# Norms by halves of the tokens: the last projections of a block and the first pairs of the next run half by half, two norms in a row folded

## The reference

```
rms(x, g)  = x * rsqrt(mean(x*x) + eps) * g
x  = x + concat(spatial gating, conformer conv, gated delta rule)(rms(x, mix_g) @ w_in) @ w_out
x  = x + (silu(rms(x, ffn_g) @ w_gate) * (rms(x, ffn_g) @ w_up)) @ w_down
x  = rms(x, final_g)                                  # end of the first block
h  = concat(meta, x)
h  = h + 0.5 * swiglu(rms(h, ffn1_g))                 # d_ff 2816
h  = h + merge(window attention, state-space scan)(rms(h, mix2_g) @ w_in_2) @ w_out_2
h  = h + 0.5 * swiglu(rms(h, ffn2_g))
out = rms(h, final2_g)[:, 16:]
```

## Time and profile before

| | |
|---|---|
| median of 3 runs | 4128.43 us (4125.76 to 4130.19) |
| profiled execution, its own time | 4125.97 us |
| its span | 4124.2 us |
| TensorE busy | 3722.5 us (90%) |
| VectorE, ScalarE, GpSimd busy | 1851.9, 598.5, 1531.2 us |
| mean granted TensorE clock | 0.952 |

### The profile page before, as it was taken

The page is one execution under the profiler, slowest core; times in us unless marked ns, Lnnn a source line. Parts: engine busy times, 40 slices in busy tenths (PEclk is TensorE's granted clock), DMA queues, the critical chain, the costliest instruction groups (busy, mean ns, idle before and its releaser), DMA issues.

```text
span 4124.2 us, 52854 instructions
## 1 busy us (share of the span) xinstructions
PE 3722.5 (90%) x20662; PEld 3162.4 (77%) x20662; DVE 1851.9 (45%) x2660; ACT 598.5 (15%) x1204; POOL 1531.2 (37%) x718
## 2 busy tenths in 40 slices
PE   5977788879999998899999979998888879999997
PEld 2756578668888886899999978887666668888886
DVE  3299566452121217422222286683777762121216
ACT  3132322110000000200000012113443010000000
POOL 3333200354444443444444453322113454444443
PEclk8989899789999999999999989999999989999998
DMA  2110000111111111111111112101002311111111
GB/s 93 36 31 26 21 1 1 61 31 46 51 45 48 45 49 43 30 42 51 41 51 46 40 47 106 55 27 44 29 24 84 117 32 46 51 41 51 46 49 63
DMA packets 56807, 189.86 MB, mean 46 GB/s; under 512 B 6112, under 2 KB 6240, under 8 KB 56032
## 3 DMA queue, kind: packets, MB, share of 16 engines
q1 hardware_dynamic: 45792, 147.20, 11.8%
q10 hardware_dynamic: 10880, 40.78, 2.6%
HBM read 170.05 MB, written 16.84 MB: 45 GB/s over the span
## 4 chain that ended last, share of the span: by engine, by line
PE 73%; DVE 20%; issue 3%; ACT 2%; POOL 1%; DMA 1%; DVEq 0%; POOLq 0%; ACTq 0%
PE acc L560 21%; PE acc L561 21%; PE acc L562 21%; DVE cv_acc L1123 2%; DVE tmp L528 2%; ACT sc L1566 1%; PE acc L846 1%; DVE ssq L648 1%; PE acc L857 1%; DVE st L1790 1%; DVE cvo L1106 1%; PE acc L856 1%; DVE sq L647 1%; PE acc L497 1%; DVE rs L518 1%
## 5 line engine op out<-in xcount | busy, mean ns | idle before, releaser
L449 POOL TENSOR_TENSOR w_hi<-w_raw,consts 128x1024 fp32r<-128x1024 f32 (+3 forms) x316 | 683.8, 2164 | 2127.8 <-PE acc L562 1861.4
L560 PE MATMUL acc<-h_hi,w_hi 128*128 128x512 f32 (+2 forms) x3552 | 1321.3, 372 | 102.4 <-issue 60.0
L561 PE MATMUL acc<-h_lo,w_hi 128*128 128x512 f32 (+2 forms) x3552 | 1320.0, 372 | 0.0
L562 PE MATMUL acc<-h_hi,w_lo 128*128 128x512 f32 (+2 forms) x3552 | 1312.6, 370 | 0.0
L560 PEld LDWEIGHTS acc<-h_hi,w_hi 128*128 128x128 f32 x3552 | 674.3, 190 | 218.5 <-issue 112.5
L561 PEld LDWEIGHTS acc<-h_lo,w_hi 128*128 128x128 f32 x3552 | 672.8, 189 | 103.4 <-issue 2.7
L562 PEld LDWEIGHTS acc<-h_hi,w_lo 128*128 128x128 f32 x3552 | 673.5, 190 | 99.2
L451 POOL TENSOR_TENSOR w_lo<-w_raw,w_hi 128x1024 fp32r<-128x1024 f32 (+3 forms) x316 | 726.0, 2297 | 24.8
L614 DVE TENSOR_TENSOR ff_hi<-tmp,acc 128x512 f32 (+3 forms) x154 | 94.5, 613 | 1119.6 <-PE acc L562 1106.0
L562 PE MATMUL acc<-ff_hi,w_lo 128*128 128x512 f32 (+2 forms) x1232 | 446.8, 363 | 0.0
L560 PE MATMUL acc<-ff_hi,w_hi 128*128 128x512 f32 (+2 forms) x1232 | 446.1, 362 | 0.0
(11 more groups left out here) (301 smaller groups left out, 3647.5 us busy)
## 6 DMA issues: line engine op xcount, KB each, us to landing
w_raw<-in_ffn_w_dram SPq DMA_DIRECT2D x88, 512.0 KB, 3.5
w_raw<-in_w_in_dram SPq DMA_DIRECT2D x56, 512.0 KB, 3.6
w_raw<-in_ffn_w_dram SPq DMA_DIRECT2D x32, 384.0 KB, 3.0
w_raw<-in_w_gate_dram SPq DMA_DIRECT2D x22, 512.0 KB, 3.5
w_raw<-in_w_up_dram SPq DMA_DIRECT2D x22, 512.0 KB, 3.5
w_raw<-in_ffn_w_dram SPq DMA_DIRECT2D x32, 320.0 KB, 2.9
w_raw<-in_w_out_dram SPq DMA_DIRECT2D x16, 512.0 KB, 3.5
gates_kept<-gstage ACTq DMA_DIRECT2D x32, 256.0 KB, 2.0
```

Source lines behind the costliest of these rows:

```text
L449: own.link(pool.tensor_tensor(hi.rearrange(blocks, n=P), raw.rearrange(blocks, n=P), ones.unsqueeze(1).broadcast_to([P, seg.kt, P]), ALU.m ...
L560: pe.matmul(bank, wh, rh, start=(k == 0), stop=False)
L561: pe.matmul(bank, wh, rl, start=False, stop=False)
L562: ins = pe.matmul(bank, wl, rh, start=False, stop=(k == seg.kt - 1))
```

## The change

- In the last segment ahead of each of the five norms (out1, the fourth down segment of each feed-forward, out2) all slabs run first for the first half of the tokens and then again for the second half; each slab is loaded and split twice. The first two pairs of the next gate/up segment (and at_u) do the same. `CH2` becomes 264, 264 and 512 columns, so that its first two chunks are the first half.
- The norm is spread over this ("turn"). Squares go to ScalarE, their sums stay on VectorE. While TensorE does the second half, VectorE and ScalarE norm the first, by the order in `TURN_DVE` ("r" reciprocal, "t" scale, "l" low part) and `TURN_HI`; the second half's norm (`TURN_REST`) runs beside the first pairs on the first half. GpSimd no longer makes `h_lo`; VectorE makes all of it.
- The two norms behind ffn0 are folded: h for ffn1 comes from the un-normed `x` with the gain `final_g * ffn1_g` and a root over squares scaled by `final_g` (with eps squared as its constant); `x` itself gets its final norm later, during ffn1's first gate/up segment and behind it (`act_fin`, `dve_fin`, `pe_fin`). The 16 meta tokens are normed during ffn0 (`dve_meta`).
- The store of `x` to `x_kept` is issued before the second root of mix2's turn. The last norm stores 512-column pieces.

```diff
-CH2 = [(0, 352), (352, 344), (696, 344)]
+CH2 = [(0, 264), (264, 264), (528, 512)]
+EARLY = 2
...
+    def halves(name, pairs, kt, chunks, src):
+        add(name + "a", pairs, kt, chunks[:-1], src)
+        add(name + "b", pairs, kt, chunks[-1:], src, lambda i, j, c: 3 * j + len(chunks) - 1)
...
+            if part == 0:
+                first, second = early_banks(chunks)
+                add(f"{name}_early_a", EARLY, KD, chunks[:-1], pair(wg, wu), first)
+                add(f"{name}_early_b", EARLY, KD, chunks[-1:], pair(wg, wu), second)
...
+                halves(f"{name}_down{part}", KD // 2, nf, chunks, run(wd[part], 0))
...
+    halves("out1", 4, KD, CH1, run(t["w_out"], 0))
...
+def turn_columns(name):
+    return (0, META + 512) if name == "mix2" else (META, 512), (META + 512, 512)
...
-        def pe_norm(pe, name, chunks):
-            pe.wait_ge(sem("ssq_" + name), 1)
-            for c, (c0, w) in enumerate(chunks):
-                pe.matmul(acc[:, c, 0:w], const("mean"), ssq[:, c0:c0 + w], start=True, stop=True)\
-                  .then_inc(sem("ms_" + name), 1)
...
-        def dve_norm_whole(dve, own, name, chunks, gain, dst):
-            for c, (c0, w) in enumerate(chunks):
-                dve.wait_ge(sem("sd_" + name), c + 1)
-                own.mark(dve.reciprocal(rs[:, c0:c0 + w], rs[:, c0:c0 + w]))
-            own.wait()
-            for k in range(KD):
-                dve.scalar_tensor_tensor(dst[:, k, META:L], x[:, k, META:L], gain[:, k:k + 1], rs[:, META:L],
-                                         ALU.mult, ALU.mult).then_inc(sem("tile_" + name), 1)
...
+                if not isinstance(i, int):
                     pe.wait_ge(acc_free[j], i * n + (seg.q0 + c + 1 - n))
-                bank = acc[:, 3 * j + c, 0:w]
+                elif seg.need[i, j, c]:
+                    pe.wait_ge(acc_free[j], seg.need[i, j, c])
+                bank = acc[:, seg.bank(i, j, c), 0:w]
...
+        def pe_mean(pe, name, half):
+            u = 2 * TURNS.index(name) + half
+            pe.wait_ge(sem("sq_added"), (KD - 1) * (u + 1))
+            if u:
+                pe.wait_ge(sem("sd_done"), parts_until(u))
+            for p, (c0, w) in enumerate(turn_parts(name, half)):
+                pe.matmul(acc[:, 6 + half + p, 0:w], const("mean"), ssq[:, c0:c0 + w], start=True, stop=True)\
+                  .then_inc(sem("ms_full"), 1)
+        def pe_ready(pe, name, half):
+            pe.wait_ge(sem("lo_done"), KD * (2 * TURNS.index(name) + half + 1))
+        def pe_last(pe, name, segs, rhs, then):
+            for half, seg in enumerate(segs):
+                if then and half == 0:
+                    for c in range(len(seg.chunks)):
+                        pe.wait_ge(sem("ff_" + then), (len(FQ) - 1) * (len(seg.chunks) + 1) + c + 1)
+                        pe_slab(pe, seg, 0, 0, rhs, only=c)
+                else:
+                    if then:
+                        pe.wait_ge(sem("ff_" + then), len(FQ) * (len(segs[0].chunks) + 1))
+                    pe_slab(pe, seg, 0, 0, rhs)
+                if half:
+                    pe_mean(pe, name, 0)
+                pe_slab(pe, seg, 0, 1, rhs)
+                with pe.Fori(1, seg.pairs) as i:
+                    for j in range(2):
+                        pe_slab(pe, seg, i, j, rhs)
+        def pe_early(pe, name, segs):
+            h, u = (h_hi, h_lo), 2 * TURNS.index(name)
+            pe_ready(pe, name, 0)
+            pe_slab(pe, segs[0], 0, 0, h)
+            pe_mean(pe, name, 1)
+            pe_slab(pe, segs[0], 0, 1, h)
+            pe.wait_ge(sem("sd_done"), parts_until(u + 2))
+            for j in range(2):
+                pe_slab(pe, segs[0], 1, j, h)
+            pe_ready(pe, name, 1)
+            for i in range(EARLY):
+                for j in range(2):
+                    pe_slab(pe, segs[1], i, j, h)
...
+        def act_turn(act, name, segs, fold=None, when_read=None):
+            def square(half, s):
+                c0, w = turn_columns(name)[half]
+                seg, v = segs[half], u + half
+                act.wait_ge(acc_free[s % 2], chunk_no(seg, s // 2, len(seg.chunks) - 1) + 1)
+                added = (KD - 1) * v + max(0, s - 3)
+                if added:
+                    act.wait_ge(sem("sq_added"), added)
+                act.activation(sq[:, s % 3, 0:w] if s else ssq[:, c0:c0 + w], x[:, s, c0:c0 + w], ACT.Square,
+                               scale=fold[:, s:s + 1] if fold is not None else 1.0).then_inc(sem("sq_full"), 1)
...
+            for s in range(KD):
+                square(0, s)
+            for s in range(KD):
+                square(1, s)
+                if s == 0:
+                    root(0)
+                for k in TURN_HI[s]:
+                    if not final:
+                        high(0, k)
+                    elif k % 2:
+                        store(0, k)
+            if when_read:
+                when_read()
+            root(1)
...
+        TURN_HI = [(), (), (0, 1, 2), (3,), (4, 5), (6,), (7,), ()]
+        TURN_DVE = [(), (("r", 0),), (("t", 0), ("t", 1), ("t", 2)), (("l", 0), ("t", 3), ("l", 1)), (("t", 4), ("l", 2), ("t", 5)),
+                    (("l", 3), ("t", 6), ("l", 4)), (("t", 7), ("l", 5), ("l", 6)), (("l", 7),)]
+        TURN_REST = [("r", 0), ("t", 0), ("t", 1), ("t", 2), ("l", 0), ("t", 3), ("l", 1), ("t", 4), ("l", 2), ("t", 5),
+                     ("l", 3), ("t", 6), ("l", 4), ("t", 7), ("l", 5), ("l", 6), ("l", 7)]
...
+            def residual(half, s):
+                seg, i, j = segs[half], s // 2, s % 2
+                for c, (c0, w) in enumerate(seg.chunks):
+                    acc_wait(dve, seg, i, j, c)
+                    xt = x[:, s, c0:c0 + w]
+                    dve.scalar_tensor_tensor(xt, acc[:, seg.bank(i, j, c), 0:w], scale, xt, ALU.mult, ALU.add).then_inc(acc_free[j], 1)
+            def add(half, s):
+                c0, w = turn_columns(name)[half]
+                dve.wait_ge(sem("sq_full"), KD * (u + half) + s + 1)
+                if u + half or s > 1:
+                    dve.wait_ge(sem("sq_added"), (KD - 1) * (u + half) + s - 1)
+                dve.tensor_tensor(ssq[:, c0:c0 + w], ssq[:, c0:c0 + w], sq[:, s % 3, 0:w], ALU.add).then_inc(sem("sq_added"), 1)
+            def piece(half, what, k):
+                v, (c0, w) = u + half, turn_columns(name)[half]
+                if what == "r":
+                    dve.wait_ge(sem("sd_done"), parts_until(v + 1))
+                    own.link(dve.reciprocal(rs[:, c0:c0 + w], rs[:, c0:c0 + w]))
+                elif what == "t":
+                    if not final and (v or k >= 3):
+                        dve.wait_ge(sem("lo_done"), KD * v + max(0, k - 2))
+                    dve.scalar_tensor_tensor(x[:, k, c0:c0 + w] if final else stage[k % 3][:, 0:w], x[:, k, c0:c0 + w], gain[:, k:k + 1],
+                                             rs[:, c0:c0 + w], ALU.mult, ALU.mult).then_inc(sem("scaled"), 1)
+                elif not final:
+                    dve.wait_ge(sem("hi_done"), KD * v + k + 1)
+                    dve.tensor_tensor(h_lo[:, k, c0:c0 + w], stage[k % 3][:, 0:w], h_hi[:, k, c0:c0 + w].bitcast(F32),
+                                      ALU.subtract).then_inc(sem("lo_done"), 1)
+            for s in range(KD):
+                residual(0, s)
+                if s > 1:
+                    add(0, s - 1)
+            add(0, KD - 1)
+            for s in range(KD):
+                residual(1, s)
+                if s > 1:
+                    add(1, s - 1)
+                for what, k in TURN_DVE[s]:
+                    piece(0, what, k)
+            add(1, KD - 1)
+            for what, k in TURN_REST:
+                piece(1, what, k)
...
+        def dve_fin(dve, own, i):
+            for e, (s, half) in fin_steps(i):
+                if s:
+                    added = e - half - 1
+                    dve.wait_ge(sem("fin_sq"), e + 1)
+                    if added:
+                        dve.wait_ge(sem("fin_added"), added)
+                    dve.tensor_tensor(ssq[:, fin_columns(half)], ssq[:, fin_columns(half)], sq[:, e % 3, 0:512],
+                                      ALU.add).then_inc(sem("fin_added"), 1)
+            if i == SEG["ffn1_up0"].pairs - 1:
+                for half in range(2):
+                    cols = fin_columns(half)
+                    dve.wait_ge(sem("fin_sd"), half + 1)
+                    own.link(dve.reciprocal(rs[:, cols], rs[:, cols]))
+                    for k in range(KD):
+                        own.mark(dve.scalar_tensor_tensor(x[:, k, cols], x[:, k, cols], param("final_g")[:, k:k + 1], rs[:, cols],
+                                                          ALU.mult, ALU.mult))
+                own.wait()
...
-            own.link(dve.memset(ssq[:, :], 0.0))
             dve.wait_ge(sem("residual_full"), 32)
-            dve_residual(dve, own, SEG["out1"], 1.0, True)
-            own.wait()
```

(59 more changed lines are left out.)

444 lines of the change are left out of this document (252 added, 192 removed).

## The result

The changed kernel takes 4148.01 us (median of 5 runs, 4146.51 to 4148.27) where the kernel before took 4128.07 beside it (5 runs). The ratio is 1.0048, with a 95% interval of 1.0033 to 1.0063: slower by about 20 us. The forecast was 4163, with a range of its own of 4140 to 4190, so the sign and the range hold and the size is 15 us too high. The span went from 4124.2 to 4145.4.

The account below looks back on a forecast made before the run. TensorE was taken as the bound, busy 90%, with 174 us lost at the norms. Terms 11 - 2 + 21 + 3 + 2 = +35 on 4125.97 gave 4161, 4163 against the median; own range 4140 to 4190, over all 4095 to 4205.

Parts of the forecast that it names:

- The lock: VectorE operations with two SBUF inputs and GpSimd's operations exclude each other for whole instructions; about 1.9 us per locked operation.
- Two of my signs: In out1b, VectorE's adds, t and l at 1.5 to 2.8 us; L449 (GpSimd's split) waiting on nothing but VectorE.
- Out1 and out2: Norms behind out1 and out2: 34 us lost against 28.7 before, so +5.4 at each.
- The losses of the first pairs: First pairs behind out1 and out2: cold starts, mean and an 11.6 us TensorE wait, 17.1 us lost.
- The first halves at 5 k-tiles: First halves of 5-k-tile segments: 3.95 us of split and hand-over per slab against 3.47 of matmuls, +3.8.
- the hand-over: Between GpSimd and TensorE at each slab on one chunk: between 0 and 0.6 us, taken as 0.4, an estimate.
- Behind ffn0: Norm behind ffn0 with folding and deferred scaling of x: 52 us lost against 54 before, -2.
- Behind ffn1: Norm behind ffn1 up to the scan: 52 to 63 us lost against 36.5 before, +21, the middle.
- The last norm: Norm at the kernel's end, no splits behind: 29.3 us against 26.1 before, +3.
- Columns: Chunks of 264, 264 and 512 columns: between -1 and +11 us by matmul pitch, taken as +2.
- VectorE keeps pace: Rival: locked operations fit beside TensorE, norms lose 80 us against 174, kernel at 4034; chance 0.17.
- The clock: Rival: clock at 1.2 GHz through gap-filled second halves, some 18 us at out1 and out2, 4199; chance 0.08.

Follow-up runs that it names:

- experiment 1: Changed kernel with GpSimd splitting only the first 128 columns of each slab in segments by halves, except out1's first half; rest left out: 4002.74 us.
- experiment 2: Changed kernel with VectorE's adds, t and l in the turns cut to 16 columns, ScalarE copying h_hi from x: 4034.38 us.
- experiment 3: Changed kernel with VectorE's adds, t and l in the turns at half width, 256 or 264 columns, h_hi copied from x: 4098.34 us.
- experiment 4: Changed kernel, everything computed, squares, stage tiles and root in PSUM at most turns, the one behind ffn1 unchanged: 4073.68 us.
- experiment 5: Changed kernel, everything computed, only the squares in PSUM at all turns but the one behind ffn1: 4133.17 us.
- experiment 7: Changed kernel with x scaled slab by slab, each before its residual of ffn1's first down segment: 4138.64 us.
- Experiment 6: Changed kernel with the scan's constants moved from behind ffn1 into ffn0's first gate/up segment: 4132.27 us.
- experiment 8: Kernel before the change with only CH2 set to chunks of 264, 264 and 512 columns: 4132.85 us.
- experiment 9: Changed kernel, everything computed, with PSUM operands, moved scan constants and slab-by-slab scaling of x together: 4051.45 us.

## Why the prediction was right in sign and 15 us too high

**How much of it is luck.** Against the table, four lines and the columns were put 18.6 us too high, and 5 us came in that I didn't have, 4.5 of them between the scan and out2. Together that is the 14 by which the span grew less; without the second the miss would have been 19.

**The lock** carried it, and it held: beside GpSimd 1.77 us an operation on average (I had 1.9), 0.68 to 0.75 when one input is in PSUM, unaffected by GpSimd. Two of my signs came out otherwise: l's mean is 1.23 us where I gave 1.5 to 2.8 for all three, since it often runs free behind one that has waited, and GpSimd's first split does wait for TensorE, 1.50 us in the rows above. The residual and the reciprocal are free of it, as taken. The Trainium skill, "SBUF — State Buffer", in the part on its two sides, says that the loser "fully blocks" for the whole instruction; by that rule the 16-column operation waits as the wide one does, and this trace agrees (1.95 and 2.35 us). By its words the lock is for two inputs in SBUF; that an operation with one of them in PSUM is free of it, the 0.68 us show. Experiments 1 to 5 show it from both sides; a bandwidth is excluded by the 1.95 us of a 16-column operation.

**Out1 and out2**, +5.4 each: +3.6 and +5.5. Ready times were right to 0.9 us. The losses of the first pairs, 17.1, went into my sum as 17.5, 0.4 too much at either norm.

**The first halves at 5 k-tiles**, +3.8 at each of three norms: the term that I had mis-sized most often. The first half takes 29.8 us behind ffn0 (1570.7 to 1600.6) and ahead of the last norm, where its matmuls need 27.8, and 30.95 for 29.2 behind ffn1: +2.1, +2.1 and +1.8. The 0.4 for the hand-over was an estimate from 8 k-tiles; a slab of 5 takes about 3.7 us and not 3.95.

**Behind ffn0**, -2: -7. Up to ffn1's first matmul on `ff_hi` the gain is 15.9, where my terms make 13 (54 less 40.9) less 2 for the means. 1.7 of the missing 4.5 is the first half above. The first half is normed 46.5 us into the second (1647.09, less the half's start at 1600.6), not 49, and the second half 37.1 later, as forecast. What let VectorE through 2.5 us sooner I haven't tested. `dve_fin` cost +8.9, of which 6.76 is the wait (I had 7 and 2.3), and experiment 7 gives 8 to 9 back.

**Behind ffn1**, +21: +16. The first half of the segment cost 2 us less than I had; it was normed 47.8 us into the second (start at 2400.5), 1.2 sooner; and then it took 76.5 us from the first half's readiness (2448.32) to bl (2524.77), where I had 72.5 to 83.5 and took the middle, 78. Two waits share it, which I had as one: 4 to 5 us of the constants' cost showed in the wait for u. Experiment 6 measures the constants at 14 to 16 us. In its trace this line takes 495.2 us, 2.1 more than before in place of 16, so the constants are nearly the whole of the loss here.

**The last norm**, +3: -1.8. This is the term that failed in sign. I walked 18.9 us from the last matmul to the end; it took 16.1 (4129.3 to 4145.4). The last sum came 2.1 us behind the start of the last residual where I had 2.7, the root was done 1.9 us behind it where I had 2.8, the eight t took 5.4 and not 5.9, the store 3.3 and not 4: each was set a little too long, and no split runs beside them. The second half in front, from 4095.4, took 33.9 us where I had 34.4, and the first half gave back 1.7 of its 3.8. The three make the 5 us.

**Columns**, +2: 0.3 us within ffn1 by experiment 8. The pitch from the earlier trace rows was right and the loads aren't a floor. What I missed in the expectation of experiment 8 is that uneven chunks change a chunk norm; the change itself has no such norm left behind ffn0.

**A term that I did not have**: +4.5 between the scan and out2, where nothing was changed but the columns. 1.6 of it lie between the scan's first matmul and the next segment, 2.8 in attention's rounds of matmuls between 2834 and 3047 us. The 1.6 belong to the scan's constants: behind the wait of 9.87 the eight matmuls on bl take 1.94 us where they took 1.06 before, those behind them are slower too, and in the kernels where that wait is 1.2 us (experiments 1, 6, 8 and 9) the stretch is as short as before. Windows of one attention round, before and after (the third number from the right is the granted clock):

```profile
2859.60:2896.80 37.20, 29.86 (x237) 22.80 (x238) 26.11 (x82) 15.84 (x58) 4.69 (x2) 0.96 0.09 30
```

```profile
2874.40:2912.80 38.40, 31.11 (x236) 23.56 (x236) 26.00 (x82) 15.86 (x58) 4.69 (x2) 0.90 0.08 28
```

The same work takes 1.2 us longer at a lower granted clock. Experiment 8 shows it too (0.90), so the halves aren't needed for it, and so do experiments 4 to 7 and 9 (0.90); experiments 1, 2 and 3 have halves and new columns as well and 0.96 there. These three are the ones that leave part of the arithmetic out. What decides it stays open.

**The rivals.** "VectorE keeps pace", which I put at 4034, isn't what happened, but it is near what kernels without the exclusion do: 4003 with few splits, which also gains in front of out2 and in attention, and 4074 with everything computed, where the turn behind ffn1 and part of the one behind ffn0 still have the lock. That experiment 2 gave 4034 is a coincidence: it still waits for the constants and the scaling. "The clock" (1.2 GHz through the second halves) did not come: from 816 to 866 us, with the gaps of 1 us in it, the granted clock is 1.00, and over the span 0.951 against 0.952.

## What to carry to other kernels

When work is moved to VectorE beside a busy GpSimd, don't count its busy time from before. Write down its chain for one slab: each operation's own time, 0.6 to 0.7 us here, and on top, for each of GpSimd's in the slab, what is left of that one when VectorE wants to start (1.6 and 2.2 us in the rows at 853.38 and 855.58). Compare the sum with the matmuls that are to cover it; here 5.6 us of cover met 7. Where banks are free, one input in PSUM takes the operation out of the waiting, and that was worth 73 us here where the change had lost 20. And when a norm is pulled forward, look at what was queued behind it: it may have been hidden by the old order, and both such pieces here (the constants, and the scaling that the change itself deferred) could be moved to where they stalled nobody.
